# mLSTM stream states updated in place in a ring of five rooms, reads behind the updates, and the last convolution rows turned inside the set-up

## The reference

```
num = (scores * weights) @ v  +  a * (q @ C^T)      # C: 512x512, the stream's state
h   = num / max(|den|, exp(-m_t))
C_new = decay * C + sum_l wg[l] * v[l] k[l]^T       # written out, 512x512
n_new = decay * n + sum_l wg[l] * k[l]
```

## Time and profile before

| | |
|---|---|
| median of 3 runs | 3936.26 us (3935.04 to 3937.03) |
| profiled execution: own time / span | 3934.65 / 3932.6 us |
| PE busy | 3504.0 us, 89% of the span |
| DVE, ACT, POOL busy | 49%, 29%, 13% |
| DMA traffic | 337.08 MB, mean 86 GB/s |
| mean granted PE clock | 0.94 of full |
| rows_out twice | about 1869 to 1891 us |
| cell_setup | 1892 to 1947.5 us |
| heads block | 1947.5 to 2011.7 us |
| streams block | 2011.7 to 2251.6 us |

### The profile page before, as it was taken

How to read it: one execution, slowest core, us unless ns; L and a number is a source line. 1 busy time by engine, 2 the same in 40 slices (tenths; PEclk the granted TensorE clock), 3 DMA queues, 4 the chain that set the end, 5 groups by cost and what they waited for, 6 DMA issues and landing times. The chain is left out here.

```text
span 3932.6 us, 53760 instructions
## 1 busy us (share of the span) xinstructions
PE 3504.0 (89%) x20489; PEld 3252.7 (83%) x20489; DVE 1917.5 (49%) x2968; ACT 1135.5 (29%) x1865; POOL 509.5 (13%) x765
## 2 busy tenths in 40 slices
PE   5549999999999989999279969997995999999997
PEld 4449989999999989999144468887995999999996
DVE  8933554445445462222533346664655444454455
ACT  5233343332232232222122212222112423322321
POOL 2240111000000120000011032221001100000000
PEclk7669999999999999999589979999997999999998
DMA  3544431111111223332289722221112111111112
GB/s 78 141 119 136 132 96 43 41 41 44 44 43 43 71 87 121 107 105 93 41 233 309 257 77 84 76 76 70 43 64 76 44 44 41 41 44 44 44 38 101
DMA packets 366173, 337.08 MB, mean 86 GB/s; under 512 B 42758, under 2 KB 293894, under 8 KB 365826
## 3 DMA queue, kind: packets, MB, share of 16 engines
q1 hardware_dynamic: 345332, 289.11, 24.1%
q0 software_dynamic: 13456, 37.61, 3.4%
q10 hardware_dynamic: 7176, 7.35, 0.6%
HBM read 231.12 MB, written 100.53 MB: 84 GB/s over the span
## 5 line engine op out<-in xcount | busy, mean ns | idle before, releaser
L1583 PE MATMUL pair<-x_head,w_head 128*128 128x384 f32 x1488 | 506.5, 340 | 54.3 <-DVE w_rest L840 30.9
L1583 PE MATMUL pair<-x_rest,w_head 128*128 128x384 f32 x1488 | 503.5, 338 | 0.0
L1583 PE MATMUL pair<-x_head,w_rest 128*128 128x384 f32 x1488 | 503.0, 338 | 0.0
L840 DVE TENSOR_TENSOR w_rest<-w_raw,w_head 128x1024 fp32r<-128x1024 f32 x228 | 291.5, 1279 | 416.6 <-ACT w_head L836 416.5
L836 ACT ACTIVATE w_head<-w_raw 128x1024 fp32r<-128x1024 f32 x228 | 242.4, 1063 | 688.6 <-PE pair L856 167.0
L1238 PE MATMUL pair<-x_head,w_head 128*128 128x384 f32 x1056 | 354.0, 335 | 10.3 <-DVE w_rest L840 8.2
L1238 PE MATMUL pair<-x_rest,w_head 128*128 128x384 f32 x1056 | 353.5, 335 | 0.0
L1238 PE MATMUL pair<-x_head,w_rest 128*128 128x384 f32 x1056 | 353.4, 335 | 0.0
L1583 PEld LDWEIGHTS pair<-x_head,w_head 128*128 128x128 f32 x1488 | 284.2, 191 | 59.2 <-issue 51.2
L1328 DVE SCALAR_TENSOR_TENSOR cv<-u,par,cv 128x1024 f32<-128x1024 f32 x88 | 112.8, 1281 | 357.7 <-ACT u L1294 357.7
L1583 PEld LDWEIGHTS pair<-x_rest,w_head 128*128 128x128 f32 x1488 | 284.3, 191 | 0.0
(11 more groups left out here) (501 smaller groups left out, 6907.8 us busy)
## 6 DMA issues: line engine op xcount, KB each, us to landing
w_raw<-in_ffn_w_up_dram SPq DMA_DIRECT2D x88, 512.0 KB, 3.8
out_dram<-hs SPq DMA_DIRECT2D x64, 512.0 KB, 7.0
w_raw<-in_s_w_glu_dram SPq DMA_DIRECT2D x48, 512.0 KB, 4.0
w_raw<-in_ffn_w_down_dram SPq DMA_DIRECT2D x44, 512.0 KB, 3.7
hs<-in_state_mlstm_C_dram SPq DMA_DIRECT2D x44, 512.0 KB, 5.8
w_raw<-in_mlstm_w_up_dram SPq DMA_DIRECT2D x32, 512.0 KB, 4.5
f<-in_state_mlstm_C_dram SPq DMA_DIRECT2D x40, 256.0 KB
xm_d<-xm SPq DMA_DIRECT2D x16, 576.0 KB, 3.9
```

The costliest lines, as they stand in the source:

```text
L840: dve.tensor_tensor(self.rest[slot][:, :], self.raw[slot][:, :], self.head[slot][:, :].bitcast(F32), ALU.subtract).then_inc(self.split, 1)
L1583: m = pe.matmul(out[:, 0:TB], lhs[slot][:, P * k:P * k + P], rhs[:, k, TB * c:TB * c + TB], start=(k == 0 and q == 0), stop=(k == KD - 1 a ...
```

## The change

Four edits. (1) The two `rows_out` calls go; `cell_setup` turns the tails with PE (bank 6 and 7) behind its first matmuls, ACT copies them into a part of `hs` that is free then, and POOL stores them and waits for the stores. (2) In the heads block SP issues the inputs of head 0 ahead of the rows of gates and the n states; the turning of n (`nrow`) moves behind the heads; three state loads move behind the writes and two more are added (rooms 3 and 4). (3) POOL loads the stacks of head 1 in the streams block, no longer in the heads block. (4) In the streams block DVE writes the new state over the old one, in a ring of five rooms (the fifth is `xc` and `xm`); all four pieces of the update stand ahead of all four reads; `cts` has two copies; within a head the streams come as 0, 2, 4, 6, 1, 3, 5, 7; SP stores step i first and then, from step 2 on, loads step i+3 into the room of step i-2, once its store has landed. The allocation edits (`FRONT_ROOM`, `tails` and `m_tails` on the right side) only make room.

```diff
@@ cell_setup
+                for k, (src, tiles, stores) in enumerate(halos):
+                    pool.wait_ge(copied, batches.index((k, 0)) + tiles // 4)
+                    for dst, r in stores:
+                        pool.dma_start(dst, stacks[k][r:r + dst.shape[0], :]).then_inc(halo_out, 16)
+                pool.wait_ge(halo_out, 16 * 4)
...
                 ins.then_inc(picked, 1)
+                for n, (k, b) in enumerate(batches):
+                    src = halos[k][0]
+                    rows_ = src.shape[2]
+                    if n >= 2:
+                        pe.wait_ge(copied, n - 1)
+                    for q in range(4):
+                        ins = pe.transpose(bank[6 + n % 2][0:rows_, P * q:P * q + P], src[:, 4 * b + q, :], env.ident[:, :])
+                    ins.then_inc(halo_turned, 1)
+                pe.wait_ge(copied, len(batches))
                 pe.wait_ge(sums, 1)
...
                 act.activation(t2[:, :], t1[:, :], ACT.Ln).then_inc(logs, 1)
+                for n, (k, b) in enumerate(batches):
+                    act.wait_ge(halo_turned, n + 1)
+                    act.activation(stacks[k][:, 4 * P * b:4 * P * b + 4 * P], bank[6 + n % 2][0:halos[k][0].shape[2], :],
+                                   ACT.Copy).then_inc(copied, 1)
@@ mlstm_streams
-        cnew, cts = [8, 12], 16
-        craw = [[strip(4 * b + t) for t in range(HT)] for b in range(2)] + [[flat(t) for t in (*cell.xc, *cell.xm)]]
+        ROOMS = 5
+        cts = [[strip(16 + k) for k in range(HT)], [flat(t) for t in (*cell.t1, *cell.t2)]]
+        craw = [[strip(4 * b + t) for t in range(HT)] for b in range(ROOMS - 1)] + [[flat(t) for t in (*cell.xc, *cell.xm)]]
...
+        order = [(h, s) for h in range(HEADS) for s in (0, 2, 4, 6, 1, 3, 5, 7)]
@@ heads block, POOL
-                    if h >= 2:
-                        pool.wait_ge(wrote[h - 2], 64)
+                    if h == 2:
+                        pool.wait_ge(wrote[0], 64)
                         for n in range(12):
-                            stack_load(pool, h - 2, n)
+                            stack_load(pool, 0, n)
@@ streams block, POOL
-                for h in range(2, HEADS):
-                    pool.wait_ge(wrote[h % 2], 128)
-                    pool.wait_ge(updated, HT * STREAMS * (h - 1))
+                for h in range(1, HEADS):
+                    pool.wait_ge(wrote[h % 2], 64 * (h // 2 + 1))
+                    if h >= 2:
+                        pool.wait_ge(updated, HT * STREAMS * (h - 1))
@@ streams block, SP
                 for i, (h, s) in enumerate(order):
+                    b = i % ROOMS
                     sp.wait_ge(updated, HT * (i + 1))
-                    if i + 3 < SR:
-                        nh, ns = order[i + 3]
-                        c_load(sp, i % 3, ns, nh)
...
+                    n = i + ROOMS - 2
+                    if i >= 2 and n < SR:
+                        sp.wait_ge(c_kept[n % ROOMS], (32 if n % ROOMS < ROOMS - 1 else 64) * (n // ROOMS))
+                        c_load(sp, n % ROOMS, order[n][1], order[n][0])
@@ streams block, PE
-                    updates(0)
-                    reads(0)
-                    updates(2)
-                    reads(2).then_inc(inter, 1)
+                    updates()
+                    for k in range(HT):
+                        ins = reads(i, k)
+                    if i % 2:
+                        ins.then_inc(inter, 1)
@@ streams block, DVE
-                    p = i % 2
-                    over(dve, c_kept[p], 32 * (i // 2))
+                    room = craw[i % ROOMS]
+                    dve.wait_ge(turned, HT * i + HT)
                     for t in range(HT):
                         dve.wait_ge(added, HT * i + t + 1)
-                        dve.scalar_tensor_tensor(out=strip(cnew[p] + t), in0=craw[i % 3][t],
+                        dve.scalar_tensor_tensor(out=room[t], in0=room[t],
@@ program
-                rows_out(env, tails, [(s_fconv[0].rearrange("s h m -> (s h) m"), 0),
-                                      (p_fconv[0, 0], STREAMS * (FTAPS - 1))], 2 * FT, (STREAMS + 1) * (FTAPS - 1))
-                rows_out(env, m_tails, [(s_mconv[0].rearrange("s h m -> (s h) m"), 0), (p_mconv[0, 0], STREAMS * MH)],
-                         IT, (STREAMS + 1) * MH)
```

More of the change, by code:

```diff
@@ L2351, in cell_setup @@
             "landed", "picked", "sums", "logs", "exps", "turned", "stored", "seeds"))
+        halo_turned, copied, halo_out = env.sem("halo_turned"), env.sem("copied"), env.sem("halo_out")
+        stacks = [room[0:halos[0][0].shape[2], 0:5, :].rearrange("r k t -> r (k t)")[:, 0:2 * FT * P],
+                  room[0:halos[1][0].shape[2], 8:10, :].rearrange("r k t -> r (k t)")[:, 0:IT * P]]
+        batches = [(k, b) for k, (src, tiles, stores) in enumerate(halos) for b in range(tiles // 4)]
         streams = lambda a: a[:, SEQ:].rearrange("h (s t) -> h s t", s=STREAMS)
@@ L2915, in mlstm_streams @@
              "summed", "d_bank4", "scored", "weighted", "v_headed", "v_split", "k_split", "cleared", "v_copied", "k_headed"))
[L2916 removed]
+        c_in = [env.sem(f"c_in{k}") for k in range(ROOMS)]
         wrote = [env.sem(f"wrote{k}") for k in range(2)]
@@ L2943, in write, with inputs @@
                         sp.dma_start(dst, src[h % 2]).then_inc(wrote[h % 2], 16)
[L2945 to L2948, removed]
+                def inputs(h):
                     over(sp, projected, h - 1)
@@ L2952, in _ @@
                             x_in[h % 2], 16)
-                    if h >= 1:
-                        c_load(sp, h - 1, h - 1, 0) if h < 3 else None
-                    if h >= 2:
-                        write(h - 2)
+                inputs(0)
+                for h in range(HEADS):
+                    sp.dma_start(row[:, h, :], rows_d[h, PCH].rearrange("k t -> (k t)").partition_broadcast(P)).then_inc(row_in, 16)
+                sp.dma_start(nrow[:, :], n_in[0].rearrange("s h k -> (s h) k")).then_inc(nrow_in, 16)
+                inputs(1)
+                inputs(2)
+                write(0)
+                c_load(sp, 0, order[0][1], 0)
+                inputs(3)
+                write(1)
+                c_load(sp, 1, order[1][1], 0)
+                c_load(sp, 2, order[2][1], 0)
                 write(2)
                 write(3)
-                sp.wait_ge(projected, HEADS)
-                c_load(sp, 2, 2, 0)
+                for n in range(3, ROOMS):
+                    c_load(sp, n, order[n][1], 0)
             @block.tensor
             def _(pe):
[L2964 to L2967, removed]
                 for h in range(HEADS):
@@ L3112, in _ @@
                         if k == 0:
-                            over(act, inter, i)
-                        act.activation(strip(cts + k), bank[k][:, :], ACT.Copy).then_inc(copied, 1)
+                            over(act, inter, i // 2)
+                        act.activation(cts[i % 2][k], bank[k][:, :], ACT.Copy).then_inc(copied, 1)
                     if s == STREAMS - 1:
-                        act.wait_ge(inter, i + 1)
+                        act.wait_ge(inter, (i + 1) // 2)
                         act.activation(flat(inter_t[h]), bank[4 + 2 * (h % 2)][:, :], ACT.Copy).then_inc(kept, 1)
```

71 lines of the change are left out of this document (42 added, 29 removed).

## The result

The changed kernel takes **3949.8 us** (median of 20 runs, 3939.8 to 3954.9), the kernel before 3936.2 us (20 runs): ratio 1.003, 95% interval 1.0023 to 1.0038. It is slower by 0.3%, 13.6 us, where 15.7 less were forecast: a gap of 29 us, and outside the range. The profiled execution of the changed kernel took 3949.6 us, its span is 3947.9.

A forecast was written before the change was run, and what follows sets the result against it. The prediction took PE to bound the streams block and POOL's stack loads to end the heads block. Terms -21.5 - 14.5 + 30.4 - 9.0 - 1.1 = -15.7 us gave 3920 us, range 3903 to 3936.

The forecast's parts named there:

- PE's clock falls in the streams block: Rival, streams block: PE's short waits for DVE bring half clock, 4.6 us more per whole step; chance 0.10.
- The chain term: Streams block: PE's later update pieces wait for DVE without reads between, +1.08 a step, net +30.4 us (26 to 34).
- The grouping of the reads: Streams block: eight read matmuls in one group save 0.1 us a step.
- rows_out: Between front and set-up: removing the block gains 21.5 us, its work moved into the set-up counted at 0.
- Heads block: Heads block: earlier head 0 inputs and twelve stack loads fewer end it at 1997 instead of 2011.5, -14.5 us (13 to 17).
- Stalls: Streams block: with in-place states and five rooms, the 9.0 us of PE stalls go, -9.0 us (0 to -9).
- End of the block: Streams block's end: last update pieces end before the reads, next block starts at 8.05 instead of 9.13 us, -1.1 us.

The follow-up runs named there:

- the interleaved kernel: Changed kernel, but each step does updates 0 and 1, reads 0 and 1, updates 2 and 3, reads 2 and 3: 3894.2 us.

## Why the prediction was wrong

**The step that failed** is the clock. The sum has no term for it: every longer step of the streams block was priced at full clock, and a share of 0.95 or more was forecast, where 0.89 was granted. The rival "PE's clock falls in the streams block (0.10): slower than before" came true. The clock cost 32.0 us in steps 0 to 31, half of the 64.6 that the new order added there. I held against that rival that the heads block was granted 0.90 with PE busy for 17.69 of 32 us. That row has other shapes: full 128-row matmuls. The runs show that PE's busy share is not what to compare: 1.34 us of waiting in a step leaves full clock, 0.83 among 48-row updates does not, and the same 0.83 among 128-row updates does. The rival's size was wrong too, in its unit: I priced whole steps at half clock, 4.6 us each. In the trace the low clock comes for short stretches and costs 1.7 us each in 17 steps. As the price of a whole step 4.6 us was too low as well: it left the updates out and took reads that were at half clock for most of their time only the earlier trace rows; the whole step at half clock in the interleaved kernel took 13.0 us, 6.1 more than 6.89.

The page of the Trainium skill named beside that rival, "TensorE: Matmul & The Clock Gate", section "A second HAM failure mode: psum-queue depth-cycling", tells of a clock that swings when PE idles briefly between groups that cycle through PSUM banks. The trace of the changed kernel agrees: its share of 0.89 is made of stretches at 1.00 and at 0.50. Such a wait alone does not bring it about: two other kernels let PE wait 0.67 and 1.34 us in each step for DVE's work on the same banks and kept 1.00.

**The chain term** (+30.4, 26 to 34) was right: 7.94 - 6.89 = 1.05 a step, 32.6 us. Piece 3 to the reads is 0.43, not 0.33. The grouping of the reads saves 0.12 (3.55 from first read to the next turning, where two groups take 3.67), forecast as 0.1. By the rule of the Trainium skill's "TensorEngine Tiling (Array Packing)", Key Properties, two mode changes fewer would have saved twice that, if each costs the same; the trace shows one such saving. That a change of mode costs time the run with 128 rows bears out: with turning and updates in one form, 1.72 instead of 1.90 us lie between their first matmuls.

**rows_out** (-21.5): right, alone -21.2. **Heads block** (-14.5): right, 48.5 us instead of 64.2 is -15.7. **Stalls** (-9.0): gone, but they are no gain of the ring: slower steps hide what the DMA needs, and with this order they go in the kernel before too. The interleaved kernel, which has the ring, waits 5.6 us for loads, and its steps 0 to 31 take 228.5 us against 227.0 before. Its whole gain of 40.7 us is that of the two parts that ran alone, 21.2 and 20.9. **End of the block** (-1.1): right, from 2256.65 (first update of the last step) to the next block's 2264.71 are 8.06 us, forecast 8.05.

With the clock's part the sum is -15.7 + 32.0 + 2.2 (chain) - 1.2 (heads) - 1.7 (the half-clock stretches and stalls before, 10.7 and not 9.0) = +15.6; the two profiled executions differ by 15.0, the medians by 13.6. Two more differences cancel in this: the set-up began 23.7 us earlier instead of 21.5, and the stages behind the streams block took 2.0 us longer (15.0 less 52.5 in the streams block, plus 15.7, 0.1 and 23.7).

What stays open: the runs fix the conditions, not the rule by which the chip weighs rows, columns and waits, nor whether the 48 rows count as such or by the change of form that they bring. Four updates without any wait were not reached (0.27 us was left), and zero-padded stacks, which would keep the result with 128 rows, weren't tried.

## What to carry to other kernels

Look at what fills the time beside a new wait, not at the wait alone: here matmuls that use few rows, standing together with waits for their PSUM banks, cost the clock as well as the wait, while the same waits beside 128-row matmuls, or a wait of up to 1.34 us ahead of reads, cost only themselves. Work that covers another engine's turn-around (here 1.84 us of reads between two pairs of updates) is worth more than it seems; one read left in between was enough to keep the clock, and cost 0.2 us a step against two. When a change has independent parts, build each alone: here two parts gained 21 us each and one lost 50.

## What the runs showed of the hardware

Two PE streams of equal order, count and waits were granted different clocks by the form of their updates: with 48 rows the clock share was 0.89, with 128 rows 1.00, and a 128-row matmul of 512 columns took no longer than a 48-row one (a pair 0.71 against 0.73 us). With 48 rows and 0.27 instead of 0.83 us of waits it was 1.00 too. In the changed kernel the half clock came over the reads behind the updates, at 1.7 us a time; with reads on both sides it also reached into the turning behind them. From the first 128x128 turning to the first update pass 1.90 us with 48 rows and 1.72 with 128.
